# The level-0 inverse X made by VectorE's 32x32 block transposition instead of a matmul with the identity

## The reference, cut to what matters

```python
def step(state, inp):
    r_t, w_t, k_t, v_t, a_t, b_t = inp
    sa = jnp.einsum('bhvk,bhk->bhv', state, a_t)
    state = (state * w_t[:, :, None, :] + sa[..., None] * b_t[:, :, None, :]
             + v_t[..., None] * k_t[:, :, None, :])
    return state, jnp.einsum('bhvk,bhk->bhv', state, r_t)
```

## Time and profile before

| | us |
|---|---|
| median of 3 runs | 4056.68 |
| lowest, highest | 4054.02, 4059.09 |
| the profiled execution | 4055.24 |
| its span | 4053.5 |
| TensorE matmuls busy in it | 3873.0 |
| VectorE, ScalarE, GpSimd busy | 1954.3, 1635.8, 1652.3 |

### The profile page before, as it was taken

The page is one execution under the profiler, slowest core; times in us unless marked ns, Lnnn a source line. Parts: engine busy times, 40 slices in busy tenths (PEclk is TensorE's granted clock), DMA queues, the critical chain, the costliest instruction groups (busy, mean ns, idle before and its releaser), DMA issues. The chain is left out here.

```text
span 4053.5 us, 67108 instructions
## 1 busy us (share of the span) xinstructions
PE 3873.0 (96%) x28244; PEld 3167.8 (78%) x28244; DVE 1954.3 (48%) x3042; ACT 1635.8 (40%) x2723; POOL 1652.3 (41%) x902
## 2 busy tenths in 40 slices
PE   8999989999999899998899999989999999999998
PEld 6888867878887788886787888777878887787887
DVE  7777673246534777767324654436231123523112
ACT  5554444343334555444434333446233224523222
POOL 4444412434445444441243444534444444444443
PEclk9999999989999899999998999989999999999999
DMA  3111113325532211111332554221222322122332
GB/s 134 48 49 44 67 45 112 104 99 188 186 131 98 85 48 49 44 68 44 111 99 97 193 183 135 99 73 43 98 89 99 98 90 79 53 94 89 99 99 83
DMA packets 108731, 379.52 MB, mean 94 GB/s; under 512 B 12561, under 2 KB 12945, under 8 KB 107793
## 3 DMA queue, kind: packets, MB, share of 16 engines
q1 hardware_dynamic: 98208, 357.27, 25.9%
q10 hardware_dynamic: 10224, 17.97, 1.2%
HBM read 359.46 MB, written 15.73 MB: 93 GB/s over the span
## 5 line engine op out<-in xcount | busy, mean ns | idle before, releaser
L293 POOL TENSOR_TENSOR Wlo<-raw,Whi 128x1024 fp32r<-128x1024 f32 x552 | 1334.4, 2420 | 1995.2 <-ACT Whi L280 1995.0
L228 PE MATMUL ps<-hh,Whi 128*128 128x512 f32 x2864 | 1152.1, 402 | 27.9 <-DVE hl L377 10.1
L228 PE MATMUL ps<-hl,Whi 128*128 128x512 f32 x2864 | 1123.4, 392 | 0.0
L228 PE MATMUL ps<-hh,Wlo 128*128 128x512 f32 x2864 | 1123.2, 392 | 0.0
L280 ACT ACTIVATE Whi<-raw 128x1024 fp32r<-128x1024 f32 x552 | 581.8, 1055 | 708.9 <-PE ps L228 607.9
L228 PEld LDWEIGHTS ps<-hh,Whi 128*128 128x128 f32 x2864 | 542.7, 189 | 160.2 <-issue 28.3
L228 PEld LDWEIGHTS ps<-hl,Whi 128*128 128x128 f32 x2864 | 543.1, 190 | 116.7 <-issue 8.6
L228 PEld LDWEIGHTS ps<-hh,Wlo 128*128 128x128 f32 x2864 | 542.2, 189 | 115.8
L228 PE MATMUL ps<-gh,Whi 128*128 128x512 f32 x864 | 337.6, 391 | 3.8 <-POOL Wlo L293 3.8
L228 PE MATMUL ps<-gh,Wlo 128*128 128x512 f32 x864 | 336.2, 389 | 0.0
L228 PE MATMUL ps<-gl,Whi 128*128 128x512 f32 x864 | 336.1, 389 | 0.0
(11 more groups left out here) (363 smaller groups left out, 5913.6 us busy)
## 6 DMA issues: line engine op xcount, KB each, us to landing
raw<-in_stream SPq DMA_DIRECT2D x554, 512.0 KB, 3.5
ada<-in_ada SPq DMA_DIRECT2D x96, 512.0 KB, 4.6
park_x<-xT SPq DMA_DIRECT2D x2, 2048.0 KB, 7.3
park_yh<-yh ACTq DMA_DIRECT2D x16, 256.0 KB, 2.1
park_yl<-yl ACTq DMA_DIRECT2D x16, 256.0 KB, 2.3
xT<-park_x SPq DMA_DIRECT2D x2, 2048.0 KB, 8.8
yrh<-park_yh ACTq DMA_DIRECT2D x16, 256.0 KB, 8.0
yrl<-park_yl ACTq DMA_DIRECT2D x16, 256.0 KB, 7.9
```

The costliest lines, as they stand in the source:

```text
L228: last = pe.matmul(ps, left[a](k), right[c](k), start=start and k == 0 and i == 0, stop=stop and k == n - 1 and i == 2)
L293: pool.tensor_tensor(b["Wlo"][:, slot], b["raw"][:, raw_slot(b, u)], b["Whi"][:, slot].bitcast(F32), SUB) \
```

## The change

VectorE now makes X of level 0. After the two XT steps of a head it writes the mask plus the identity, with the halves not crossed, to Wc (steps i0, i1), and transposes Wc in blocks of 32x32 into X (steps X00, X01). Level 0 has entries only within 2x2 blocks, so blocks of 32 hold all of it. TensorE's 16 small products a pair and ScalarE's two copies are gone. W of level 1 waits for VectorE. GpSimd's masks of level 2 wait for the transposition instead of the product. VectorE's mixing of r stays ahead of the XT steps, the mixing of k and the scan behind them.

```diff
-INV_P = Steps("X00", "X01", *[f"{m}{l}{h}" for l in range(1, LEVELS) for m, h in
+INV_P = Steps(*[f"{m}{l}{h}" for l in range(1, LEVELS) for m, h in
...
-INV_A = Steps("d00", "d01", "d10", "d11", "X00", "X01", *[f"W{l}{h}" for l in range(1, LEVELS) for h in range(2)])
-INV_V = Steps("t00", "T00", "t01", "T01", *[f"{m}{l}{h}" for l in range(1, LEVELS) for h in range(2) for m in "XT"
+INV_A = Steps("d00", "d01", "d10", "d11", *[f"W{l}{h}" for l in range(1, LEVELS) for h in range(2)])
+INV_V = Steps("t00", "T00", "i0", "t01", "T01", "i1", "X00", "X01", *[f"{m}{l}{h}" for l in range(1, LEVELS) for h in range(2) for m in "XT"
...
@@ rwkv_inv_pe
-    for h in range(2):
-        pe.wait_ge(s["inv_v"], INV_V(p, f"T0{h}"))
-        for c in range(BLK):
-            for u in range(2):
-                last = pe.matmul(b["ps"][half(1 - u), 4 + h, block(c)], b["XT"][half(u), h, block(c)], b["c"]("identc")[half(u)],
-                                 start=True, stop=True)
-        last.then_inc(s["inv_p"], 1)
...
-            if l > 1:
-                pe.wait_ge(s["inv_v"], INV_V(p, f"X{l - 1}{h}"))
-            else:
-                pe.wait_ge(s["inv_a"], INV_A(p, f"X0{h}"))
+            pe.wait_ge(s["inv_v"], INV_V(p, f"X{l - 1}{h}"))
@@ rwkv_inv_act
-    for h in range(2):
-        act.wait_ge(s["inv_p"], INV_P(p, f"X0{h}"))
-        act.activation(b["X"][:, h], b["ps"][:, 4 + h, 0:BLK * CB], ACT.Copy).then_inc(s["inv_a"], 1)
@@ rwkv_inv_pool
-                    pool.wait_ge(s["inv_p"], INV_P(p, f"W{l - 2}{h}") if l > 2 else INV_P(p, f"X0{h}"))
+                    pool.wait_ge(*((s["inv_p"], INV_P(p, f"W{l - 2}{h}")) if l > 2 else (s["inv_v"], INV_V(p, f"X0{h}"))))
@@ rwkv_inv_dve
+        dve.tensor_tensor(blocks(b["Wc"][:, h]), blocks(b["TM"][:, h, 0]), ident, ADD).then_inc(s["inv_v"], 1)
+    for h in range(2):
+        dve.wait_ge(s["inv_v"], INV_V(p, f"i{h}"))
+        dve.transpose(b["X"][:, h], b["Wc"][:, h]).then_inc(s["inv_v"], 1)
```

## The result

| | before | after |
|---|---|---|
| median, us | 4057.89 (4054.02 to 4059.52) | 4090.98 (4084.27 to 4100.89) |
| the profiled execution, us | 4055.24 | 4084.27 |
| its span, us | 4053.5 | 4082.5 |

A forecast was written before the change was run, and what follows sets the result against it. TensorE's own work was taken to bound the stage: 14 pairs gaining 1.25 us minus two last pairs losing 0.25 make 17.0 us, so 4055.24 becomes 4038.2, as a median 4039.7 us; range 4035 to 4045.

The forecast's parts named there:

- What bounds the kernel now: In the pairs' stage, TensorE is busy 54.78 of 55 us without listed waits, so removing its work shortens the stage.
- Term 1: At level 0 on TensorE, removing X0 saves 1.25 us in each of 16 pairs, 20.0 us, if X is ready.
- Rivals A to C: Price of one transposition: two passes, 0.68 us, 4041.9 (with forecast 0.77); 0.9 to 1.4, 4058.5 (0.07); 1.5, 4068.1, slower (0.04).
- Term 2: Each layer's last pair gains nothing and loses 0.25 us at W of level 1, leaving 17.0 us in all.
- Who else is moved: Later VectorE and earlier GpSimd work stays covered; otherwise pair 0 loses up to 1 us per layer, the others nothing.
- With two of 0.3, the scan ends at about 204.7.: VectorE after the transpositions: two meetings with GpSimd's masks cost 0.3 us each, making the level-1 X sum 1.5 late.
- That split moves up with ScalarE, so VectorE's delay is swallowed there.: At VectorE's 2.31 us cm step, which ends 0.54 after GpSimd's second weight split, the delay costs nothing.
- It is wanted by W of level 2 ... so 2.4 remain: The level-1 X sum, started at 204.7, is wanted at 207.5: 2.4 us to spare, about 1 in pair 0.
- Rival D: The pairs' gain is given back or absorbed, as by W of level 2 waiting: 4046.7 to 4056 us; chance 0.12.

The follow-up runs named there:

- kernel 7: The change, with GpSimd's level-2 masks waiting for VectorE's last scan step and its second weight split behind the level-4 masks: 4037.68 us, ratio 0.9955.
- kernel 8: The change, with level-2 masks behind the scan, VectorE's order bonus multiply, kkr, then cm, fe, cum, and ScalarE's exponentials waiting for cum: 4037.05 us, ratio 0.9949.
- experiments 1 to 6: The change with GpSimd's masks or split, or VectorE's bonus multiply, moved; the second instead adds VectorE's new steps to the kernel before: 4055.66 to 4074.89 us.
- experiment 9: Kernel 7 with each transposition made twice, the second overwriting the first: 4046.49 us, ratio 0.9978.

## Why the prediction was wrong, by its own steps

**Right.** "What bounds the kernel now": TensorE's stream sets the stage, and every us that its waits lose is in the total. **Term 1** at its own place: GV to W 1.08 us, in 14 pairs. The worth of it, once nothing else was late, is 1.25 us a pair (54.74 to 53.49, experiments 7 and 8). The transposition: 0.42 us forecast, and the group's mean is 421 ns (two in a row overlap and take 0.76, so that the mixing of k began 1.5 us later and not 1.8):

```profile
L1108 DVE STREAM_TRANSPOSE X<-Wc 128x256 f32<-128x256 f32 x16 | 6.1, 421 | 0.0
```

Rivals A to C, all about its price, did not come up. As forecast, i0 took the stall, 2.54 us where 2.51 stood in the earlier trace rows. **Term 2**: W of level 1 in the last pairs 2.58 and 2.59 behind GV instead of 2.34, so +0.24 and +0.25 where 0.25 was forecast.

The Trainium skill ("SBUF — State Buffer", section on the two separate sides of SBUF) says that a GpSimd instruction that reads SBUF and a VectorE one with two SBUF inputs exclude each other for the whole instruction, and so do a GpSimd instruction and a VectorE one in a faster mode that uses both ports. The traces agree: i0 2.54, a scan 2.55 and kkr 2.58 us each end 0.27 to 0.29 behind a split, and the X sums are not held. Of the transposition only 0.25 us lie beside a mask, too little to tell.

**The step that failed is "Who else is moved".** It named the right engines, with the wrong durations, and it stopped one step short. In detail:

- *"With two of 0.3, the scan ends at about 204.7."* That is 4.5 us behind GV. Seen: 7.55 behind GV. Two mixing steps did cost 0.43 and 0.35. But the scan was left at its own 1.36, and it has two SBUF inputs like the XT step of the earlier trace rows. With the masks lasting to 208.70, its first two met them and took 0.95 and 0.88 us, and the third met the split. The row for the price was in the prediction: 2.51 beside a split, in place of 0.42.
- *"That split moves up with ScalarE, so VectorE's delay is swallowed there."* The split did move, from 4.93 to 4.45 behind GV: it comes directly behind the masks. It had been good for VectorE at its old place, since it held only cm, which had time for it. Moved by half a us, while the scan moved by 2.3 (0.73 to 3.00), it holds a scan instead. The rows of both were there, and the prediction never laid the new scan beside the new split.
- *"It is wanted by W of level 2 ... so 2.4 remain"* was about the right slack for the first of two waits. It was read in pair 2, where W of level 2 starts 8.57 us behind GV; in the other pairs from 1 to 6 it starts at 8.37, which leaves 2.2. The X sum stands 7.47 us behind GV where 4.5 was forecast: 2.9 more, against 2.2 to spare, and TensorE waits 0.8. In pair 0, where about 1 us was to remain, it waits 1.6.
- **Left out altogether**: the bonus multiply. Before, it ends 9.78 us behind GV and TensorE's mean product takes it at 10.63, a slack of 0.85. In pair 2 of layer 1, which the rows show, the mean product stands 0.2 later, at 10.83 (GV at 200.17). The prediction did not look at these rows:

```profile
209.27 0.68 DVE L1161 TENSOR_TENSOR rk<-ps,v 128x512 f32<-128x512 f32 x1
...
211.00 1.12 PE L840 MATMUL ps<-y,const 128*128 128x512 f32 x2
```

  With TensorE 1.25 us earlier, this step at its old place would already be 0.4 us late. It did not stay there but went 2.5 us back (9.78 to 12.29). That there is a second wait, and a nearer one than W of level 2, was to be had from two such rows by subtraction; its size only with the scan's. In pair 0, which has no bonus multiply, ScalarE's Wc of level 3 was the second wait (1.6 us, 0.3 before), and the prediction left that out too.

**Rival D** named the mechanism ("GpSimd's earlier masks hold back the mixing so that W of level 2 waits") and bounded it at 1 us in half of the pairs, ending at no change. Seen were 2.62 us in 12 pairs and 3.2 in each pair 0, with the clock on top. It was held down by "TensorE's wait list is empty, so I see no taker". An empty list says that nothing is late now; it doesn't say by how much.

**The size.** 12 x 2.94 (waits and what is lost beside them) + 2 x 3.3 (the same in pair 0) + 4 x 1.6 (clock) + 2 x 0.25 - 14 x 1.25 = 35.3 + 6.6 + 6.4 + 0.5 - 17.5 = 31.3, against 30.9 measured in the two stages (11.9 + 18.5 and the last pairs' 0.5) and 29.0 in the whole (two pairs of the kernel before took 55.1 and 55.2 us, which lowers the difference by 0.8). What the forecast of 4039.7 describes does exist: it is kernel 7, 4037.68, or kernel 8, 4037.05, both some 20 us faster than the kernel before and some 53 faster than the change.

## What to carry to other kernels

When work is taken out of the bounding engine's stream, list for every later wait of that engine in the period how early its releaser is now, and compare the smallest of these slacks with the gain: here 0.85 against 1.25 already told of a wait. When a step is moved in time, lay it and all that follows it on its engine beside the other engine that shares its port, instruction by instruction, and charge a meeting with the longest instruction there and not with the mean. If they meet, the cure is the order (what is wanted soon goes first, what blocks goes behind it) and not less work.

## What the runs showed of the hardware

- A one-input step can be held too: kkr (a tensor by a scalar per partition, 512 columns in 0.47 us where a two-input step takes 0.68) took 2.58 us beside a split of 2.80. A short step can be held as long: fe, with two inputs of three columns each, took 2.21 beside a split and 0.16 alone. The X and XT sums, with one operand in PSUM, were not longer beside GpSimd's masks (0.39 to 0.42).
- A meeting costs both sides: four masks take 2.82 us beside little and 3.02 to 3.82 beside VectorE's steps, the split 2.5 to 2.8 instead of 2.39.
- The 32x32 transposition of 128x256 in float32 takes 0.42 us in the mean, and each further one in a row adds 0.33 (two 0.76, four 1.42).
- Two idle times of TensorE, of 0.8 and 1.8 us, were followed by the lower clock (0.50 granted, some 3.3 us long) in 4 and 6 of the 12 pairs that had them, in two executions, at the same place of the pair. In the other 8 and 6 they were not, nor were the two of 1.6 us in pair 0 of these executions. With hardly any idle time in the pairs (before, kernels 7 and 8) it was not seen there. It also fell behind single waits of 1.3 to 2.7 us (in pair 0 of experiments 1 to 6, in the last pair of experiment 9). What decides between the pairs is not settled.
